# Norms of a two-block transformer kernel: how their sums of squares and reciprocal roots are ordered over three engines

## The reference, cut to what matters

```python
def rmsnorm_2(t, g):
    tf = t.astype(jnp.float32)
    y = tf * lax.rsqrt(jnp.mean(tf * tf, axis=-1, keepdims=True) + EPS)
    return (y * g.astype(jnp.float32)).astype(t.dtype)

def gla_output(o, r, norm_g):
    of = o * lax.rsqrt(jnp.mean(o * o, axis=-1, keepdims=True) + EPS) * norm_g.astype(jnp.float32)

# in layernorm of the convolution:  xc * lax.rsqrt(jnp.mean(xc * xc, axis=-1, keepdims=True) + EPS)

x = x + g1 * (jnp.concatenate([gla_lat, sc_lat, na_lat], axis=-1) @ w_out[layer])
h = modulate(rmsnorm_2(x, norm_ffn_g[layer]), sh2, sc2)          # h feeds the up projection
x = x + g2 * conv_ffn(h, ...)
```

## Time and profile before

| | us |
|---|---|
| median of 3 runs | 1439.65 |
| lowest and highest of them | 1438.21, 1441.66 |
| span of the profiled execution | 1438.0 |
| TensorE matmuls busy in it | 1373.6 |
| VectorE busy | 1049.1 |
| ScalarE busy | 708.4 |

### The profile page before, as it was taken

One profiled execution on the slowest core, in us unless ns is written; L12 is line 12 of the kernel. 1 busy time (PEld: TensorE's weight loads), 2 busy tenths in 40 slices (PEclk: granted clock), 3 DMA queues, 4 the chain that ended last, 5 costly groups with the idle time before them and its releaser, 6 DMA issues.

```text
span 1438.0 us, 21914 instructions
## 1 busy us (share of the span) xinstructions
PE 1373.6 (96%) x8493; PEld 1183.3 (82%) x8493; DVE 1049.1 (73%) x2008; ACT 708.4 (49%) x1193; POOL 48.0 (3%) x67
## 2 busy tenths in 40 slices
PE   6999999999999999898999999999999988899997
PEld 5777987879978886677888888888888867899997
DVE  6697786978779885737788998666643765788854
ACT  6537666366544642734434344322345735566643
POOL 0000000000000012000000000000000110000000
PEclk9999999999999999998999999999999999999999
DMA  7643556325376531031454455577333322355553
GB/s 265 220 161 120 160 179 221 132 89 191 118 267 226 163 100 48 16 117 44 142 166 161 150 166 169 184 253 257 124 116 118 118 89 69 126 188 180 184 187 96
DMA packets 61943, 218.52 MB, mean 152 GB/s; under 512 B 7024, under 2 KB 9072, under 8 KB 61456
## 3 DMA queue, kind: packets, MB, share of 16 engines
q1 hardware_dynamic: 59200, 205.55, 43.5%
q0 software_dynamic: 2496, 11.56, 2.3%
q10 hardware_dynamic: 144, 0.00, 0.0%
HBM read 216.04 MB, written 1.05 MB: 151 GB/s over the span
## 4 chain that ended last, share of the span: by engine, by line
PE 81%; ACT 7%; DVE 7%; issue 2%; DMA 2%; DVEq 0%; SPq 0%; ACTq 0%
PE bank L583 20%; PE bank L584 19%; PE bank L585 19%; PE bank L599 5%; ACT WHI L1450 2%; DVE WLO L2010 2%; DMA RAWB<-in_ws 2%; PE bank L1271 1%; ACT L1450 1%; PE bank L644 1%; DVE DP L2109 1%; PE bank L646 1%; PE bank L645 1%; PE bank L621 1%; PE bank L622 1%
## 5 line engine op out<-in xcount | busy, mean ns | idle before, releaser
L583 PE MATMUL bank<-NHI,WHI 128*128 128x256 f32 (+1 forms) x1392 | 463.2, 333 | 8.6 <-DVE WLO L2010 7.0
L2010 DVE TENSOR_TENSOR WLO<-RAWB,WHI 128x1024 fp32r<-128x1024 f32 (+1 forms) x276 | 328.6, 1193 | 180.8 <-ACT WHI L1450 179.8
L584 PE MATMUL bank<-NLO,WHI 128*128 128x256 f32 (+1 forms) x1392 | 457.4, 329 | 0.0
L585 PE MATMUL bank<-NHI,WLO 128*128 128x256 f32 (+1 forms) x1392 | 457.4, 329 | 0.0
L1450 ACT ACTIVATE WHI<-RAWB 128x1024 fp32r<-128x1024 f32 (+1 forms) x276 | 283.1, 1029 | 192.1 <-PE bank L585 113.3
L583 PEld LDWEIGHTS bank<-NHI,WHI 128*128 128x128 f32 x1392 | 264.3, 190 | 42.7 <-issue 10.5
L584 PEld LDWEIGHTS bank<-NLO,WHI 128*128 128x128 f32 x1392 | 264.4, 190 | 24.6 <-issue 1.4
L585 PEld LDWEIGHTS bank<-NHI,WLO 128*128 128x128 f32 x1392 | 264.4, 190 | 23.4
L2109 DVE CUSTOM_DVE_ANT_0 DP<-RAWB,CREP,PRM 128x1024 f32<-128x1024 f32 x120 | 154.0, 1283 | 9.4 <-DMA RAWB<-in_ws 3.9
L1450 ACT ACTIVATE CF<-bank,PRM 128x512 f32<-128x512 f32 (+1 forms) x88 | 59.1, 671 | 177.1 <-PE bank L585 174.7
L583 PE MATMUL bank<-HHI,WHI 128*128 128x256 f32 (+1 forms) x330 | 110.4, 335 | 0.0
(11 more groups left out here) (355 smaller groups left out, 1957.6 us busy)
## 6 DMA issues: line engine op xcount, KB each, us to landing
RAWB<-in_ws SPq DMA_DIRECT2D x364, 512.0 KB, 3.4
RAWB<-in_ws SPq DMA_DIRECT2D x32, 384.0 KB, 3.6
NB<-in_nab POOLq DMA_DIRECT2D x12, 256.0 KB, 3.6
CREP<-in_crep POOLq DMA_DIRECT2D x2, 1024.0 KB, 6.4
K<-in_c POOLq DMA_DIRECT2D x2, 896.0 KB, 5.8
K<-in_c POOLq DMA_DIRECT2D x1, 1344.0 KB, 8.8
X<-in_xt SPq DMA_DIRECT2D x4, 256.0 KB, 5.3
X<-in_xt POOLq DMA_DIRECT2D x1, 1024.0 KB, 6.9
```

The costliest lines, as they stand in the source:

```text
L583: nc.tensor.matmul(o, hi[:, w], xh, start=(i == 0), stop=False)
L584: nc.tensor.matmul(o, hi[:, w], xl, start=False, stop=False)
L585: ins = nc.tensor.matmul(o, lo[:, w], xh, start=False, stop=(i == slabs - 1))
L2010: V.tensor_tensor(WLO[:, k % SPL, 0:w], RAWB[:, u % RAW, 0:w], WHI[:, k % SPL, 0:w].bitcast(F32), ALU.subtract).then_inc(S("lo_ready"), 1)
```

## The change

Seven edits, all in the norms:

1. `residual` on both engines is reordered: ScalarE squares a pair ahead of the splits at that slab's `rest()`, and VectorE gathers ahead of them as well.
2. The add of slab 6 (L2051) goes. TensorE sums three slabs instead of two.
3. At five places (behind both output projections and both feed-forward parts of the second block, and between the blocks) the function table is fetched early: `load_root_table` issues one activation of a 128x1 constant into `UNREAD`, which nothing reads. In `residual` it stands after the last split and ahead of the last two squares, between the blocks ahead of the wait for the sums.
4. The guess reads the bank itself, with EPS as a bias from a new constant column `eps`; the instruction that added EPS goes. It waits for `ms_ready` instead of `ms_eps`.
5. One Newton step of three instructions instead of two steps; its first instruction reads the bank and adds EPS.
6. For 512 tokens the roots are spread in two banks, latent in 4 and context in 5, each with its own `r_spread`.
7. The waits of the other norms (convolution, first block, heads, halves) are rewritten to fit.

```diff
@@ tensor: half_sums and stats_behind
-                for k in (0, last):
+                for k in (0, last - 1, last):
                     if k == 0:
                         pe.wait_ge(S("sq_gathered"), me.nth("sq_gathered"))
                     else:
-                        me.nth("sq_ready", KS // 2)
-                        pe.wait_ge(S("sq_ready"), me.nth("sq_ready"))
+                        pe.wait_ge(S("sq_ready"), me.nth("sq_ready", 1 if k == last else KS // 2))
@@ tensor: after the output projection of the second block
-                spread_scales("r_tok", "r_spread", n // P)
-                held[4] = (S("t_ready"), me.nth("t_ready", KS * seqs))
+                spread_scales("r_tok", "r_spread")
+                if uc:
+                    pe.wait_ge(*held[5])
+                    for t in range(TT):
+                        ins = nc.tensor.transpose(bank[5][:, t * P:(t + 1) * P], GR[:, 3, TT + t:TT + t + 1].broadcast_to([P, P]), cst("ident"))
+                    ins.then_inc(S("r_spread"), 1)
+                held[4] = held[5] = (S("t_ready"), me.nth("t_ready", KS * seqs))
@@ scalar
-            def guess(m, g, given):
+            def guess(m, g, given, bias=0.0):
 
                 act.wait_ge(S(given), me.nth(given))
-                A(g, m, ACT.Abs_reciprocal_sqrt).then_inc(S("rs_guess"), 1)
+                A(g, m, ACT.Abs_reciprocal_sqrt, bias=bias).then_inc(S("rs_guess"), 1)
+
+            def load_root_table():
+
+                A(UNREAD[:], cst("eps"), ACT.Abs_reciprocal_sqrt)
@@ scalar: residual
-                    if m < KS:
-                        rest(1 if halves and m == KS - 1 else units)
                     if m >= 3 and m % 2 == 1 and m < KS:
                         act.wait_ge(S("wo_freed"), me.nth("wo_freed", 2))
                         if m - 3 >= ring:
                             act.wait_ge(S("sq_used"), 2 * summed[0] + (m - 5) // 2)
                         squares(n, sq, m - 3, min(m - 3, ring - 2))
+                    if m < KS:
+                        rest(1 if halves and m == KS - 1 else units)
+                    if m == KS:
+                        load_root_table()
@@ scalar: one of the guesses
-                guess(GR[:, 0, 0:n // P], GR[:, 2, 0:n // P], "ms_eps")
+                guess(bank[4][:, 0:n // P], GR[:, 2, 0:n // P], "ms_ready", cst("eps"))
@@ vector
-            def rsqrt(m, g, t, out, done="dve_chain", beside=None):
+            def rsqrt(m, eps, read, g, t, out, done="dve_chain", beside=None):
 
                 dve.wait_ge(S("rs_guess"), me.nth("rs_guess"))
-                for o, last in ((g, "dve_chain"), (out, done)):
-                    V.scalar_tensor_tensor(t, m, -0.5, g, ALU.mult, ALU.mult).then_inc(S("dve_chain"), 1)
-                    if beside is not None:
-                        beside(o is out)
-                    dve.wait_ge(S("dve_chain"), me.nth("dve_chain"))
-                    V.tensor_tensor(t, t, g, ALU.mult).then_inc(S("dve_chain"), 1)
-                    dve.wait_ge(S("dve_chain"), me.nth("dve_chain"))
-                    V.scalar_tensor_tensor(o, t, 1.5, g, ALU.add, ALU.mult).then_inc(S(last), 1)
-                    dve.wait_ge(S(last), me.nth(last))
+                V.scalar_tensor_tensor(t, m, eps, g, ALU.add, ALU.mult).then_inc(S(read), 1)
+                if beside is not None:
+                    beside(0)
+                dve.wait_ge(S(read), me.nth(read))
+                V.scalar_tensor_tensor(t, t, -0.5, g, ALU.mult, ALU.mult).then_inc(S("dve_chain"), 1)
+                if beside is not None:
+                    beside(1)
+                dve.wait_ge(S("dve_chain"), me.nth("dve_chain"))
+                V.scalar_tensor_tensor(out, t, 1.5, g, ALU.add, ALU.mult).then_inc(S(done), 1)
+                dve.wait_ge(S(done), me.nth(done))
@@ vector: add_squares, slab 6 no longer added
-                    V.tensor_tensor(sq[:, 0, 0:n], sq[:, 0, 0:n], sq[:, 1, 0:n], ALU.add).then_inc(S("dve_chain"), 1)
-                    dve.wait_ge(S("dve_chain"), me.nth("dve_chain"))
-                    dve.wait_ge(S("sq_ready"), me.nth("sq_ready"))
-                    V.tensor_tensor(sq[:, 0, 0:n], sq[:, 0, 0:n], sq[:, sq.shape[1] - 2, 0:n], ALU.add).then_inc(S("sq_gathered"), 1)
-                    me.nth("sq_ready")
+                    V.tensor_tensor(sq[:, 0, 0:n], sq[:, 0, 0:n], sq[:, 1, 0:n], ALU.add).then_inc(S("sq_gathered"), 1)
+                    me.nth("sq_ready", 2)
@@ vector: residual
                 for m in range(KS):
+                    add_squares(m, n, sq)
                     if halves and m == KS - 1:
                         rest()
-                        add_squares(m, n, sq)
...
                     rest(units)
                     for _ in range(dots[m] if dots else 0):
                         dot()
-                    add_squares(m, n, sq)
```

More of the change, by code:

```diff
@@ L1515, in shift_by_halves @@
             def shift_by_halves(l, shift, beside_hidden, sq, sq_at, root_at, rests, split_at=None):
-                guess(GR[:, 0, 0:TT], GR[:, 2, 0:TT], "ms_eps")
+                guess(bank[4][:, 0:TT], GR[:, 2, 0:TT], "ms_ready", cst("eps"))
                 if -1 in rests:
@@ L1528, in shift_by_halves @@
                     if i == root_at:
-                        guess(GR[:, 0, TT:], GR[:, 2, TT:], "ms_eps")
+                        guess(bank[5][:, 0:TT], GR[:, 2, TT:], "ms_ready", cst("eps"))
                     act.wait_ge(S("t_ready"), me.nth("t_ready"))
@@ L1608, in _ @@
                 rest(2 if l == 0 else 1)
-                guess(GR[:, 0, 0:TT], GR[:, 2, 0:TT], "ms_eps")
+                if l == 0:
+                    act.wait_ge(S("ld_cst"), 16)
+                guess(bank[4][:, 0:TT], GR[:, 2, 0:TT], "ms_ready", cst("eps"))
                 if l > 0:
@@ L1697, in _ @@
                     if l > 0 and t == CTX_SUMS_AT + 1:
-                        guess(GR[:, 0, 0:TT], GR[:, 2, 0:TT], "csum_eps")
+                        guess(bank[4][:, 0:TT], GR[:, 2, 0:TT], "csum_ready", cst("eps"))
                     if t == 3:
@@ L1741, in _ @@
                 silu("pgate", 2, 2)
-                guess(MS1[:, 0, :], MS1[:, 2, :], "cvar_eps")
+                act.wait_ge(S("cstat_ready"), me.nth("cstat_ready"))
+                guess(bank[5][:, 0:T], MS1[:, 2, :], "cstat_ready", cst("eps"))
                 def ple(u, tiles):
@@ L1792, in _ @@
             rest()
+            load_root_table()
+            me.seen["ms_eps"] = DEPTH
             guess(GR[:, 0, :], GR[:, 2, :], "ms_eps")
+            me.nth("ms_ready")
             act.wait_ge(S("x_split"), me.nth("x_split", KS * DEPTH))
@@ L1945, in end_of_gated @@
                     if i == 0:
-                        guess(GS[:, 0, 0:12 * seqs], GS[:, 2, 0:12 * seqs], "oms_eps")
+                        guess(bank[4][:, 0:12 * seqs], GS[:, 2, 0:12 * seqs], "oms_ready", cst("eps"))
                     if i == 1:
@@ L2157, in _ @@
                 rest(2 if l == 0 else 1)
-                dve.wait_ge(S("ms_ready"), me.nth("ms_ready"))
-                V.tensor_scalar(GR[:, 0, 0:TT], bank[4][:, 0:TT], EPS, None, ALU.add).then_inc(S("ms_eps"), 1)
-                rsqrt(*(GR[:, i, 0:TT] for i in (0, 2, 1, 3)), "r_tok")
+                rsqrt(bank[4][:, 0:TT], EPS, "ms_eps", *(GR[:, i, 0:TT] for i in (2, 1, 3)), "r_tok")
                 if l > 0:
@@ L2482, in root @@
                     g = slice(TT * c, TT * (c + 1))
-                    dve.wait_ge(S("ms_ready"), me.nth("ms_ready"))
-                    V.tensor_scalar(GR[:, 0, g], bank[4 + c][:, 0:TT], EPS, None, ALU.add).then_inc(S("ms_eps"), 1)
-                    rsqrt(*(GR[:, i, g] for i in (0, 2, 1, 3)), "r_tok", beside)
+                    rsqrt(bank[4 + c][:, 0:TT], EPS, "ms_eps", *(GR[:, i, g] for i in (2, 1, 3)), "r_tok", beside)
                 def scaled(i):
@@ L2791, in end_of_gated @@
                 def end_of_gated(i):
-                    if i == 0:
-                        output_eps()
                     if i == 1:
-                        rsqrt(*(GS[:, j, 0:6 * nt] for j in (0, 2, 1, 3)), "ors_ready")
+                        rsqrt(bank[4][:, 0:6 * nt], EPS, "oms_eps", *(GS[:, j, 0:6 * nt] for j in (2, 1, 3)), "ors_ready")
                     if i == 2:
```

30 lines of the change are left out of this document (13 added, 17 removed).

## The result

| | us |
|---|---|
| changed kernel, median of 4 runs | 1431.38 (1430.77 to 1434.81) |
| kernel before, median of 4 runs | 1439.95 (1438.21 to 1441.66) |
| ratio | 0.9936, 95% interval 0.9921 to 0.9952 |
| span of the profiled execution | 1429.8 |

The change is faster by 8.6 us (by the ratio 9.2). The direction was forecast, the size was not: the sum gave 5.15 us and the time lies 0.4 us under the stated range. One of the six runs of e13, a later repeat of the changed kernel, took 1701.42 us in a slower state of the chip and is left out of what follows.

What follows compares the result with a forecast made beforehand. TensorE was taken as the bound, with 81% of the chain. Terms 1.9 + 1.0 + 1.0 + 0.9 + 0.6 - 0.25 = 5.15 us, off the median 1439.65, gave 1434.5 us, range 1431.8 to 1437.4.

Steps and rivals of the forecast that it cites:

- The direction: Whole kernel: faster, meaning under 1436.8 us, was given a chance of 0.78.
- the sum: Whole kernel: the gains and costs at all norms added up to 5.15 us saved.
- the stated range: Whole kernel: time from 1431.8 to 1437.4 us, to leave out no more than 2 in 10.
- The waits of the two output projections and the end: Gains of 1.0 us after the first output projection, 1.9 after the second and 1.0 at the kernel's end.
- The ceiling of 2.1: Second output projection: no more than 2.1 us can come through, the following split leaving only 0.2 us of lead.
- The split that I took for fixed: Behind the second output projection: split ending at 1243.96 us, for a unit TensorE takes at 1244.17.
- the rival of half: Both output projections: the low clock halves the gains to 1.0 and 0.5 us, total 3.75, time 1435.9; chance 0.18.
- The convolution's norm: Convolution's norm in both layers: 0.6 us gained together, ends 0.3 and 0.75, against a TensorE wait of 0.39.
- The halves: Halves after the first feed-forward part: a cost, -0.25 us, ends 0 and -0.5.
- The price of the third slab: Halves: a third slab summed by TensorE costs 0.95 us for both together, beside an idle 1.04.
- The place of the tiles: Tile places in memory: no term of the prediction names them, so no gain or cost was counted.
- Head norms: Head norms in two layers: 0.9 us gained for both, ends 0.5 and 1.2, from one Newton step less.

Runs made afterwards that it cites:

- e13: Repeat of the changed kernel, nothing altered: 1433.78 us, ratio 0.9944 to the kernel before.
- e6: Changed kernel without the early activation that fetches the function table, each load standing ahead of its guess: 1433.5 us, ratio 0.9947 to the kernel before.
- e10: Changed kernel with squares and adds behind the splits again, the seventh slab still summed by TensorE: 1433.09 us, ratio 0.9951 to the kernel before.
- e11: Changed kernel with squares and adds behind the splits again and slab 6 added by VectorE again: 1433.27 us, ratio 0.9951 to the kernel before.
- e5: Changed kernel with a second Newton step of three instructions back in every root: 1438.41 us, ratio 0.9986 to the kernel before.
- e1: Kernel before with only one unused 32-byte tile declared ahead of PICK, moving HHI and HLO: 1440.09 us against 1440.92, ratio 0.9996.
- e15: Repeat of the kernel before with the 32-byte shift alone: 1440.03 us, ratio 0.9996 to the kernel before.
- e16: Kernel before, norms untouched, with WHI and WLO laid out 64 bytes off for 256 columns of NHI: 1430.46 us, ratio 0.9928 to the kernel before.
- e14: Repeat of the changed kernel without the shift, all tiles where they lay before: 1433.68 us, ratio 0.9952 to the kernel before.
- e2: Changed kernel with UNREAD put into unused columns of PICK, so all tiles lie where they lay before: 1435.73 us, ratio 0.9963 to the kernel before.
- e8: Changed kernel with WHI/WLO slots 128 bytes longer and units for 256 columns (and HHI's 512) 64 bytes further on: 1430.48 us, ratio 0.9928 to before.
- e3: Changed kernel with 64 bytes more declared ahead of PICK: 1432.63 us, ratio 0.9944 to the kernel before.

## Why the prediction was wrong

- **The waits of the two output projections and the end: right.** 1.2, 2.1 and 1.07 us for 1.0, 1.9 and 1.0. e6, e10 and e11 give the parts of the second: 0.6 for the table, 0.6 for the order, 0.4 for the seventh slab, and e5 0.6 for Newton. The ceiling of 2.1 that I set there was no ceiling. TensorE's next unit began at 1244.17 and now begins at 1238.84; of these 5.33 us the stage had 3.06 of lead (1229.00 to 1225.94), which leaves 2.3. The split that I took for fixed stands behind the norm's own products in VectorE's list and moved 2.2 us with them (1242.73 to 1237.47).
- **The clock: the rival of half was wrong.** From the first matmul of the up projection to the 49th it takes 7.81 us before and 7.74 or 7.75 in all nine new traces behind the second output projection, so nothing of the gain was lost there. Behind the first it takes 13.45 before and 13.26 in e1, e15 and e16; four of the new traces have 13.26 as well, the other five 13.50 to 13.82, the changed kernel's own 13.66. There the clock takes 0.2 of the 1.2 us on average, and half a microsecond at most.
- **The convolution's norm: mis-sized, 0.6 for both layers where 1.0 was measured.** I capped it at the bracket of 0.39 us. A bracket counts from the end of the matmul before, which is 0.28 long, while matmuls back to back start 0.12 apart; so a wait of 0.39 delays the next start by 0.39 + 0.28 - 0.12 = 0.55. The wait is gone in the changed kernel, and the group ahead of it, which waits for ScalarE's `PL`, takes back some 0.07.
- **The halves: the wrong sign, -0.25 where +0.24 was measured. This is the step that failed.** The price of the third slab was right: without it (e11) the stage is 0.45 us shorter, and the rest of its 0.9 went into the idle 1.04. What I overlooked is the other side, 0.7 us that the stage gains even so (14.95 before, 14.26 in e11): I did not ask whose queue the sum was read in. Before, the EPS instruction stood behind a split on VectorE; now ScalarE reads the bank while that split runs. The kernel before, then the changed one:

```profile
1035.38 0.96 DVE L2010 TENSOR_TENSOR WLO<-RAWB,WHI 128x768 fp32r<-128x768 f32 x1 [0.92 <-ACT WHI L1450]
...
1036.25 0.15 DVE L2484 TENSOR_SCALAR GR<-bank 128x2 f32<-128x2 f32 x1
1036.44 0.20 ACT L1450 ACTIVATE GR<-GR 128x2 f32<-128x2 f32 x1 [1.09 <-DVE GR L2484]
```

```profile
1031.04 1.40 PE L708 MATMUL bank<-PICK,SQF 128*128 128x2 f32 x12
...
1031.87 0.96 DVE L2027 TENSOR_TENSOR WLO<-RAWB,WHI 128x768 fp32r<-128x768 f32 x1 [0.91 <-ACT WHI L1455]
...
1032.47 0.26 ACT L1455 ACTIVATE GR<-bank,CST 128x2 f32<-128x2 f32 x1 [0.63 <-PE bank L708]
...
1033.77 0.44 PE L796 MATMUL bank<-WHI,NHI 128*128 128x384 f32 x1 [0.18 <-DVE NLO L2507]
```

Before, the sum was there 1 us ahead of the guess; now the guess follows it by 0.03 us (1031.04 + 1.40 = 1032.44), and the wait of 1.04 is 0.18. No run puts the EPS instruction back alone, so this cause is read from the rows; e5 gives 0.24 of the 0.7 to the Newton step.
- **The place of the tiles: put at nothing without a reason, and also a step that failed.** A 128x1 tile that nothing reads moved `HHI` by 32 bytes and made its matmuls faster, 1.8 us by the trace once `ZH` is taken off. In the time it is worth 0.6 us (e1, e15), 1.2 (e13 against e14, by the ratios) or 3.9 (the result against e2, each by its own ratio); only its pace is shown, its share of the gain stays open between these.
- **Head norms: right, a little small.** 0.6 and 0.56 us for 0.45 each. The brackets alone don't tell it, because the wait falls now ahead of the attention's matmuls, now ahead of the root: the first layer's reads 1.48 us before and next to nothing in the changed kernel.

The norms alone, 5.3 and 6.9 us in two measurements, are near the 5.15 of the sum and the 6.8 of the stage table. By the table the sum was 1.6 us short: 0.5 at the halves, 0.4 at the convolution, 0.3 at the heads, 0.4 at the output projections and the end. What the result holds beyond, up to 1.8 us, is of the size that the place has in the trace. The last 0.4 us outside the range are no more than scatter: e13, the same kernel measured again, took 1433.78 beside 1441.2 of the kernel before, and lies inside it.

## What to carry to other kernels

Where a change moves a read of PSUM from one engine to another, look at what stands ahead of the read in both lists: the gain can be a split that is no longer waited for, not the instruction saved. When TensorE is never idle, count its matmuls in a window of fixed length before and after; where the pace differs with equal code, look at where the tiles lie, and at a second execution of the same program. Measure stages from anchor to anchor over several traces, with the first anchor ahead of all work that the change adds; half a microsecond can be read there that no median shows.

## What the runs showed that was not expected

Back to back fp32r matmuls don't run at one pace here. For `HHI` and `NHI`, by the distance between the multiplied tile and its weights in a partition as worked out from the declarations: 0 bytes 120.0 ns for 256 columns and 226.7 for 512; 32 bytes 117.3 and 234.3; 64 bytes 113.3 and 233.3, once mostly 117 to 118. For 512 columns a distance of 128 bytes is not as good as 0 (232.3 in e8), one of 256 is. Using this alone took 10 us off the kernel before, and with the norms 20. It is no full law: by the same working `ZH` lies 64 bytes off in the kernel before and runs at 118.0 ns, 96 off in the changed one at 120.0, and 32 off in e3 at 117.8.
